# Memory attention: maxima and exponentials read from PSUM, the root by logarithm and exponential, and the values' product in the loop's first passes

## The reference

```
q = (xn @ w_cq).reshape(bsz, s, X_HEADS, X_HEAD_DIM)
kv = (memn @ w_ckv).reshape(bsz, memn.shape[1], 2, X_HEADS, X_HEAD_DIM)
k, v = kv[:, :, 0], kv[:, :, 1]
sc = jnp.einsum('bshd,bmhd->bhsm', q, k).astype(jnp.float32) * (1.0 / math.sqrt(X_HEAD_DIM))
p = jax.nn.softmax(sc, axis=-1)
o = jnp.einsum('bhsm,bmhd->bshd', p.astype(v.dtype), v).reshape(bsz, s, X_HEADS * X_HEAD_DIM)
return o @ w_co
```

## Time and profile before

| what | value |
|---|---|
| median of 3 runs | 2346.13 us (2341.47 to 2346.25) |
| profiled execution | 2338.41 us, its span 2336.6 us |
| mean granted TensorE clock | 0.959 |
| TensorE busy | 2143.8 us, 92% of the span |
| VectorE busy, ScalarE busy | 895.4 us (38%), 556.2 us (24%) |
| HBM traffic over the span | 149 GB/s |

### The profile page before, as it was taken

The page is one execution under the profiler, slowest core; times in us unless marked ns, Lnnn a source line. Parts: engine busy times, 40 slices in busy tenths (PEclk is TensorE's granted clock), DMA queues, the critical chain, the costliest instruction groups (busy, mean ns, idle before and its releaser), DMA issues.

```text
span 2336.6 us, 38044 instructions
## 1 busy us (share of the span) xinstructions
PE 2143.8 (92%) x15826; PEld 1198.9 (51%) x15826; DVE 895.4 (38%) x1512; ACT 556.2 (24%) x948; POOL 250.4 (11%) x252
## 2 busy tenths in 40 slices
PE   6988999787979989999999999978899999999997
PEld 3445556464434444654446454545655666665553
DVE  2116520763564440485446562156431111111114
ACT  3023312333641210242113211024101111111112
POOL 0005410551320000000000000000010000000002
PEclk9999999887999999999999999989799999999999
DMA  8130111103022024102110301100379999999995
GB/s 304 50 127 19 41 59 36 50 19 131 1 90 36 37 90 142 37 1 73 36 36 1 135 1 72 39 9 28 121 290 397 415 408 410 414 409 410 411 367 223
DMA packets 100149, 348.98 MB, mean 149 GB/s; under 512 B 18632, under 2 KB 48992, under 8 KB 87264
## 3 DMA queue, kind: packets, MB, share of 16 engines
q1 hardware_dynamic: 56496, 267.64, 29.4%
q0 software_dynamic: 14688, 54.53, 6.3%
q10 hardware_dynamic: 28880, 25.66, 3.3%
HBM read 308.75 MB, written 39.06 MB: 149 GB/s over the span
## 4 chain that ended last, share of the span: by engine, by line
PE 34%; DMA 11%; DVE 5%; ACT 2%; issue 1%; ACTq 0%; another core or an unknown queue 0%; DVEq 0%; SPq 0%; PEldq 0%
PE bank L586 16%; DMA y_of_slot<-HT 10%; PE bank L1158 8%; PE bank L1174 4%; PE bank L997 2%; DVE work L1721 1%; ACT work L1268 1%; DMA work<-in_w_e_up_dram 1%; PE bank L642 1%; PE bank L1164 1%; DVE O L1727 1%; PE bank L1149 1%; DVE HT L1756 0%; PE bank L582 0%; ACTq L1649 0%
## 5 line engine op out<-in xcount | busy, mean ns | idle before, releaser
L586 PE MATMUL bank<-slots,HT 128*128 128x512 f32 (+3 forms) x1216 | 428.0, 510 | 3.4 <-DVE HT L1756 1.7
L586 PE MATMUL bank<-HT,slots 128*128 128x512 f32 x736 | 320.6, 598 | 3.8 <-PEq L576 1.3
L586 PEld LDWEIGHTS bank<-slots,HT 128*128 128x128 f32 x1216 | 214.4, 196 | 196.6 <-issue 187.9
L1268 ACT ACTIVATE work<-work 128x1024 f32<-128x1024 f32 (+7 forms) x207 | 168.9, 827 | 284.7 <-DVEq L141 198.8
L1268 ACT ACTIVATE work<-bank 128x512 f32<-128x512 f32 (+5 forms) x215 | 114.5, 538 | 506.7 <-PE bank L586 353.4
L586 PEld LDWEIGHTS bank<-HT,slots 128*128 128x128 f32 x736 | 140.9, 192 | 181.9 <-issue 177.1
L1268 ACT ACTIVATE HT<-bank 64x256 f32<-64x256 f32 (+2 forms) x234 | 100.7, 436 | 462.9 <-PE bank L1158 209.0
L1158 PE MATMUL bank<-slots,HT 128*32 128x256 f32 x3264 | 179.5, 379 | 2.2 <-DVE HT L2343 1.2
L2423 POOL TENSOR_TENSOR work<-work 128x1024 f32<-128x1024 f32 (+4 forms) x84 | 137.1, 1632 | 373.7 <-DVEq L141 307.8
L1158 PE MATMUL bank<-work,HT 128*32 128x256 f32 x3072 | 168.9, 379 | 0.8 <-DMA work<-in_w_e_up_dram 0.7
L1158 PEld LDWEIGHTS bank<-slots,HT 128*32 128x32 f32 x3264 | 107.4, 110 | 72.1 <-issue 5.4
(11 more groups left out here) (259 smaller groups left out, 2373.2 us busy)
## 6 DMA issues: line engine op xcount, KB each, us to landing
slots<-in_w_e_gate_dram SPq DMA_DIRECT2D x17, 2048.0 KB, 18.1
slots<-in_w_e_up_dram SPq DMA_DIRECT2D x17, 2048.0 KB
slots<-in_w_e_down_dram SPq DMA_DIRECT2D x17, 2048.0 KB, 23.5
work<-in_w_e_gate_dram SPq DMA_DIRECT2D x16, 2048.0 KB, 18.1
work<-in_w_e_up_dram SPq DMA_DIRECT2D x16, 2048.0 KB
work<-in_w_e_down_dram SPq DMA_DIRECT2D x16, 2048.0 KB, 23.5
slots<-in_w_in_dram SPq DMA_DIRECT2D x9, 2048.0 KB, 9.0
y_of_slot<-HT ACTq DMA_DIRECT2D x132, 96.0 KB, 1.9
```

Of the source, the lines that this page charges most:

```text
L586: ins = pe.matmul(bank, lhsT, rhs, start=(n == 0), stop=(n == len(pairs) - 1))
L1268: return act.activation(o, i, f, bias=bias, scale=scale, **more)
```

## The change

Five things are altered. (1) The fourth tile of the queries' product is computed after the memory's turning instead of before it, and VectorE empties in that order. (2) ringA gets banks 0 to 2, ringV banks 3, 6 and 7; banks 4 and 5 are kept for the scores, with two semaphores of their own: `scores_full` (a bank is written) and `scores_free` (its exponentials are done). (3) VectorE takes the maxima straight from these banks and negates them; ScalarE makes four exponentials of 128x256 from them, with the negated maximum as bias and the row's sum as a second output; the copies, the subtraction and the sum on VectorE are gone. (4) The two fills of the values' product stand behind scores 0 and scores 1 in the loop, and their copies behind the exponentials of these passes. (5) The root is exp(-0.5 ln(v)) instead of the square root of a reciprocal, with one preload of a table set that has both functions. The wait for the output weights stands in the loop, before their use.

```diff
--- before.py
+++ after.py
@@ -469,6 +469,10 @@
             OT = cut(ar(4 * T), 4)
             assert ar.at <= 15 * T
             return CQ, M2, MT, CK, CV, S, PT, OT
+
+
+        scores_full, scores_free = sem("memory_scores_full"), sem("memory_scores_free")
+        SCORE_BANKS = banks[4:6]
 
 
         TAIL = 3 * NK * HALF
@@ -1062,33 +1066,37 @@
 
 
             CQ, M2, MT, CK, CV, S, PT, OT = cross_area()
-            product_fm("cross_q", 512, fm_fills(4))
+            product_fm("cross_q", 512, [fill for fill in fm_fills(4) if fill[0] < 3])
             hear("dve")
             for f in range(NK):
                 bank = ringV.open(pe)
                 for q in range(2):
                     ins = pe.transpose(bank[:, q * P:(q + 1) * P], M2[:, q, f * P:(f + 1) * P], const("ident"))
                 ringV.close(ins)
+            product_fm("cross_q", 512, [fill for fill in fm_fills(4) if fill[0] == 3])
             emptied()
+            ringA.use(banks[0:3])
+            ringV.use([banks[3], banks[6], banks[7]])
             w = weights("cross_k")
             for m in range(4):
                 ringA.close(chain(ringA.open(pe)[:, 0:MEM], [(w[:, k, m * P:(m + 1) * P], MT[:, k, :]) for k in range(NK)]))
             used("cross_k")
-            product_tm("cross_v", 512, [(i, ringA) for i in range(2)], x=MT)
-            emptied()
+            pe.wait_ge(ringA.free, ringA.filled)
             attended, turned_banks = [], []
             n = chunk_of["cross_out"] % 3
-            weights("cross_out")
             w_co_slot = cut(slots[:, n * NK * HALF:(n + 1) * NK * HALF], 4)
             for n in range(NT + 3):
                 if n < NT:
-                    for x in range(2):
-                        bank = ringV.open(pe)
+                    for x, bank in enumerate(SCORE_BANKS):
+                        if n:
+                            pe.wait_ge(scores_free, 2 * (n - 1) + x + 1)
                         for y in range(2):
                             h = 2 * x + y
                             ins = pe.matmul(bank[:, y * MEM:(y + 1) * MEM], CQ[:, h, n * P:(n + 1) * P], CK[:, h, :],
                                             start=True, stop=True)
-                        ringV.close(ins)
+                        ins.then_inc(scores_full, 1)
+                if n < 2:
+                    product_tm("cross_v", 512, [(n, ringA)], x=MT)
                 if 1 <= n <= NT:
                     b = n - 1
                     hear("dve")
@@ -1102,6 +1110,7 @@
                 if 2 <= n <= NT + 1:
 
                     pe.wait_ge(ringA.free, attended[n - 2])
+                    weights("cross_out")
                     for half in range(2):
                         ringV.close(chain(ringV.open(pe), [(OT[:, k, (n - 2) * P:(n - 1) * P],
                                                             w_co_slot[:, k, half * HALF:(half + 1) * HALF])
@@ -1610,17 +1619,28 @@
             for m, half, ring in fm_fills(4):
                 if ring is ringA:
                     empty(lambda b: func(CQ[:, m, half * HALF:(half + 1) * HALF], b, ACT.Copy, scale=P ** -0.5))
+            act.preload_act_table_set("natural_log_exp_and_others")
             for m in range(4):
                 empty(lambda b: func(CK[:, m, :], b[:, 0:MEM], ACT.Copy))
-            for i in range(2):
-                empty(lambda b: func(CV[:, i, :], b, ACT.Copy))
             for n in range(NT + 3):
                 if n < NT:
                     hear("dve")
-                    do(S[n % 2], S[n % 2], ACT.Exp)
+                    for x, bank in enumerate(SCORE_BANKS):
+                        for y in range(2):
+                            h = 2 * x + y
+                            at = 4 * (n % 2) + h
+                            ins = func(S[n % 2][:, h, :], bank[:, y * MEM:(y + 1) * MEM], ACT.Exp, bias=mx[:, at:at + 1],
+                                       accum_out=rden[:, at:at + 1])
+                        line(ins, scores_free)
                     tell("dve")
+                if n < 2:
+                    empty(lambda b: func(CV[:, n, :], b, ACT.Copy))
                 if n >= 3:
-                    take_root(n - 3)
+                    r = rstd[:, n - 3:n - 2]
+                    hear("dve")
+                    do(r, r, ACT.Ln)
+                    do(r, r, ACT.Exp, scale=-0.5)
+                    roots.tell(act)
                 if 1 <= n <= NT:
                     for x in range(2):
                         empty(lambda b: func(PT[:, 4 * x:4 * x + 4, :], cut(b, 4), ACT.Copy))
@@ -2184,30 +2204,33 @@
             tell("pe")
             for m, half, ring in fm_fills(4):
                 if ring is ringV:
+                    if m == 3:
+                        for f in range(NK):
+                            empty(lambda b: dve.tensor_scalar(MT[:, f, :], b[:, 0:MEM], normcols["norm_mem_2"][:, f:f + 1],
+                                                              None, ALU.mult))
                     empty(lambda b: dve.tensor_scalar(CQ[:, m, half * HALF:(half + 1) * HALF], b, P ** -0.5, None, ALU.mult))
-            for f in range(NK):
-                empty(lambda b: dve.tensor_scalar(MT[:, f, :], b[:, 0:MEM], normcols["norm_mem_2"][:, f:f + 1], None,
-                                                  ALU.mult))
             for n in range(NT + 3):
                 if 1 <= n <= NT:
                     s = S[(n - 1) % 2]
                     m = slice(4 * ((n - 1) % 2), 4 * ((n - 1) % 2) + 4)
                     hear("act")
-                    line(dve.tensor_reduce(rden[:, m], s, AX_X, ALU.add))
                     line(dve.reciprocal(rden[:, m], rden[:, m]))
                     tt(s, s, bcast(rden[:, m].unsqueeze(2), [P, 4, MEM]), ALU.mult)
                     tell("pe")
                 if n < NT:
-                    s = S[n % 2]
                     m = slice(4 * (n % 2), 4 * (n % 2) + 4)
-                    for x in range(2):
-                        empty(lambda b: dve.tensor_copy(s[:, 2 * x:2 * x + 2, :], cut(b, 2)))
-                    line(dve.tensor_reduce(mx[:, m], s, AX_X, ALU.max))
-                    tt(s, s, bcast(mx[:, m].unsqueeze(2), [P, 4, MEM]), ALU.subtract)
+                    for x, bank in enumerate(SCORE_BANKS):
+                        at = 4 * (n % 2) + 2 * x
+                        dve.wait_ge(scores_full, 2 * n + x + 1)
+                        line(dve.tensor_reduce(mx[:, at:at + 2], cut(bank, 2), AX_X, ALU.max))
+                    ts(mx[:, m], mx[:, m], -1.0, None, ALU.mult)
                     tell("act")
                 if n >= 3:
                     i = n - 3
-                    root_at(i)
+                    roots.hear(dve)
+                    ts(rstd[:, i:i + 1], ss[:, i:i + 1], 1.0 / D, EPS, ALU.mult, ALU.add)
+                    tell("act")
+                    roots.hear(dve)
                     if i >= 3:
 
                         hear("pool")
```

## The result

The changed kernel takes 2310.32 us (median of 4 runs, 2308.23 to 2315.48) against 2346.19 us (2341.47 to 2348.11) for the kernel before. The medians differ by 35.9 us. The estimate of the ratio on record is 0.9865 with a 95% interval of 0.9845 to 0.9884, which is 31.7 us, between 27 and 36.

A forecast was written before the change was run, and what follows sets the result against it. TensorE, busy 92% of the span, was taken as the bound, so gains come from its idle time or slow clock. 0.66 + 13.8 + 6.3 + 0.75 = 21.5, plus 1.5 for the clock, 23.0 us: 2346.1 to 2323.1, range 2315 to 2332.

The forecast's parts named there:

- the clock in front: At the memory's turning before the keys' product: a clock that stays up gains 1.5 us, bounds 0 and 3.1.
- The loop's beginning: The values' product behind scores 0 and 1 covers TensorE's waits and keeps its clock up: 13.8 us.
- The product's wait of 0.15 us: Before each product of weights and values TensorE waits for ScalarE's copies; five such waits go: 0.75 us.
- DVE's sum in the chain: Before five turnings of weights, DVE's sum of 1.26 us leaves the chain TensorE waits for: 6.3 us.
- The tail: From the last turning to the first expert's load: no gain counted in the sum beyond the shorter wait.
- In the loop the idle time of 2.13 us left the turn behind it fast: Waits before the weights' turnings: 2.13 us idle kept the clock up, while 6.95 and 3.86 us made turns slow.
- Maxima, exponentials, root, rings: In each pass: 0.69 us per maximum, 0.58 per exponential with its read; root off the path, fewer banks cost 0.
- The base: The whole kernel's time from which the gain was taken: 2346.1 us, the median of the runs shown.
- the clock stays up at both places: Rival, chance 0.18: full clock before the keys' product and at the last turn; gain 26.2 us, time 2319.9.

The follow-up runs named there:

- Experiment 3: The changed kernel with both fills of the values' product and their copies put back before the loop; 2323.28 us, ratio 0.9914 to the kernel before.
- after: The changed kernel with all five alterations, against the kernel before; 2310.32 us, ratio 0.9865.
- experiment 4: The changed kernel with the sums of the exponentials put back on VectorE; 2325.51 us, ratio 0.9911 to the kernel before.
- experiment 8: The kernel before with only idle products added in TensorE's waits, no wait shortened; 2337.57 us, ratio 0.9979 to the kernel before.
- 6: The kernel before with only the values' product's two fills, and their copies, moved behind scores and exponentials 0 and 1; 2331.82 us, ratio 0.9951.
- experiment 5: The changed kernel with the square root and VectorE's reciprocal put back; 2316.20 us, ratio 0.9874 to the kernel before.

## Why the prediction was wrong, point by point

Two things put the time below the range: the attention gained 5.6 us more than the sum of 23.0, and the base from which the sum was taken off was too high. The stretch's gain of 28.6 us by the prediction's own terms, from the two first profiles:

| part | forecast | measured |
|---|---|---|
| up to the keys' product's start | 0.66 | 0.7 |
| keys' product to scores 0, without the values | 1.5 | 3.06 |
| scores 0 to turning 3, without the values | 15.2 | 16.3 |
| turning 3 to turning 7 | 5.6 | 6.7 |
| turning 7 to the first expert's load | 0 | 1.8 |
| sum | 23.0 | 28.6 |

- **The step that failed first is the clock in front**: "I take half, 1.5 us". With 3.54 us of transposes between two long products the clock did not come down in any of the eight profiles that have this order (keys' product 14.05 us in each). With the 5.22 us from the turning's start to the keys' start, 1.68 of them idle at the end, it was down in all five that have this order without idle products (15.7 to 17.1 us). The whole 3.06 us were to be had. The Trainium skill says that a transpose doesn't count as busy time for the clock in the way other products do ("TensorE: Matmul & The Clock Gate", Part 4: PE-mode transpose), and the prediction drew from it that this place might gain nothing. The measurement went against that inference. It doesn't test the rule, since the same transposes ran in both orders and only what stood around them changed.
- **The loop's beginning** was right in mechanism: 6.95 us covered, 1.07 us left (forecast 1.1), the slow clock gone. Experiment 3 shows that the move was needed for it, although the chain had become shorter; my expectation there was half of what was measured. Of the 1.1 us by which this row exceeds the forecast, 0.4 is a wait before turning 2 that the prediction didn't count. It is gone in after and back when DVE sums again (experiment 4):

```profile
1563.90 1.09 PE L1099 MATMUL bank<-cst,work 128*128 128x128 f32 x8 [0.24 <-DVEq L141]
```

Another 0.3 is the product's wait of the next point. The last 0.3 lies before turning 0, where the two halves of the values' product take up 13.7 us and not 13.9.
- **The product's wait of 0.15 us** was mis-sized. From one output product's start to the next product's it is 7.18 us in the earlier trace rows (1579.73 to 1586.91) and 6.86 in after (1580.80 to 1587.66): the wait costs 0.32 us, its recorded length and the overlap of the two records that it prevents. The product behind it then takes 2.05 us instead of the 1.95 of after, so each wait cost 0.42 us and not 0.15. Four passes make 1.1 us, all that turning 3 to turning 7 gained beyond the forecast.
- **DVE's sum in the chain** was right: 2.13 to 0.87 us at four turnings, 3.86 to 2.60 at the last. Experiment 4 brings these back (2.13 and 3.85).
- **The tail** was put at 0 and gained 1.8 us. Before, router products 4 and 5 are one row of 4.05 us, the turning behind them takes 1.95 and router product 6 takes 3.63:

```profile
1664.26 4.05 PE L586 MATMUL bank<-slots,HT 128*128 128x36 f32 x32
1668.12 1.95 PE L642 MATMUL bank<-cst,work 128*128 128x128 f32 x8
1670.92 3.63 PE L586 MATMUL bank<-slots,HT 128*128 128x36 f32 x16 [0.86 <-DVE HT L1756]
```

In after these are 3.66, 1.07 and 3.06 us, as the clock fell later. The row of 3.66 us stands in every profile with the exponentials from the banks, and 4.0 to 4.1 us in the three with the old code and no idle products. But the kernel before with idle products (experiment 8) has 3.66 too, so the shorter work on DVE and ScalarE isn't needed for it. Why the clock fell later isn't settled.
- **"In the loop the idle time of 2.13 us left the turn behind it fast"** was true of the one trace and doesn't hold in general: experiments 4 and 6 have two falls each behind such waits.
- **Maxima, exponentials, root, rings** were right: 0.69 us for a maximum, 0.47 + 0.19 us for an exponential, nothing for the root, and nothing for the banks as long as the values' product stands between scores 0 and 1 (2.23 us without it).
- **The base.** 12.8 us lie between forecast and median, and 5.6 of them are the attention. With the attention right, the forecast would have been 2346.1 - 28.6 = 2317.5 us, still 7.2 above the measured median. The 2346.1 us were the median of three runs; the later medians of the same kernel, of 15 to 20 runs, are 2340.3 to 2343.2 us, 3 to 6 lower. The prediction counted the spread among its three runs but not that their median could lie high. What is left, 1 to 4 us, may be the experts' stretch, 2.5 us shorter in the first profile of after and 2.8 in the second. It is not the change: with the same code there it took between 622.6 (experiment 8, code of before) and 629.1 us (experiment 5). What sets it stays open, as does what moves the part upstream.

Of the rivals, 'the clock stays up at both places' (0.18) came nearest with 26.2 us, but is only half true: the clock did fall at turning 7 after a wait of 2.60 us, 1.97 us there. Its number is near by luck, since it left out the 1.8 us of the tail and what was mis-sized in the waits.

## What to carry to other kernels

A wait has two prices: its length, and the slow products behind it if the clock falls. Here filling the waits with idle long products gave 7 us in the stretch, though no wait became shorter; in the time of the whole kernel it is hard to see (ratio 0.9979, up to 0.9995). Where a profile shows one execution, read the stretch around the change between two fixed events and compare that; spans and single runs moved by 8 to 17 us for reasons outside the change, and the median of three runs lay 3 to 6 us above those of 15 to 20. Even the stretch needs its parts ahead of the change looked at, which moved by 1.6 us. And after a chain has been shortened, ask whether its head still stands behind something else in the engine's order: moving the multiplication up into the pass before gave another 7 to 10 us in the stretch.

## What was not expected of the hardware

- A wait of 2.13 us, with short products and transposes ahead and transposes behind, was followed by a fall of the clock in some passes and not in others, in the same execution (two of four in experiments 4 and 6, none of four before); one product took 8.73 us there instead of 7.03.
- Identical code ahead of the attention does not take the same time in every execution: over the 14 profiles the load of the queries' weights comes between 1297.3 and 1301.7 us in six and between 1306.0 and 1308.4 in the other eight. Where compared, the windows differ in granted clock (0.89 and 0.71 between 160 and 200 us).
- In an accumulating exponential of 128x256 from PSUM the activation takes 0.47 us, some 0.08 more than the copy of the earlier trace rows, and the accumulator's read of 0.19 us overlaps it by 0.1 us: four take 2.07 us. The pointer to the bias may be the reason; no run here changed it alone. The Trainium skill gives about 93 ns for each such operand ("ScalarE: Activation LUTs", What ACT_TABLE_LOAD costs).
